# Making the low parts of the mixer's weight tiles on GpSimd in place of VectorE

## The reference, cut to what matters

```python
h = h + FFN_RES * swiglu(rmsnorm(h, ffn1_norm[layer]), ffn1_w_gate[layer], ffn1_w_up[layer], ffn1_w_down[layer])
h = h + token_mixing(rmsnorm(h, mix_norm[layer]), w_in[layer], lb_all[layer], hg_norm[layer],
                     conv_w[layer], conv_b[layer], conv_ln_g[layer], conv_ln_b[layer], w_out[layer])
h = h + FFN_RES * swiglu(rmsnorm(h, ffn2_norm[layer]), ffn2_w_gate[layer], ffn2_w_up[layer], ffn2_w_down[layer])
...
def token_mixing(u, ...):
    z = u @ w_in
    ...
    o = gla_chunk_scan(qs, ks, vs, gs)
    ...
    glu = z[..., 5 * W:5 * W + C] * jax.nn.sigmoid(z[..., 5 * W + C:5 * W + 2 * C])
    c = depthwise_conv(glu, conv_w, conv_b)
    ...
    return jnp.concatenate([hg_out, c], axis=-1) @ w_out
```

## Time and profile before

| | |
|---|---|
| median of 3 runs | 2802.3 us (2797.23, 2802.3, 2803.67) |
| span of the profiled execution | 2799.2 us, first to last instruction |
| a time of its own for the profiled execution | none is listed beside the three; its span is 3.1 us under their median |
| one pass of the loop over heads | about 157 us, three passes from about 1108 to 1580 us |
| low parts made in the four heads | 28 of the 171 in the program |

### The profile page before, as it was taken

One profiled execution on the slowest core, in us unless ns is written; L12 is line 12 of the kernel. 1 busy time (PEld: TensorE's weight loads), 2 busy tenths in 40 slices (PEclk: granted clock), 3 DMA queues, 4 the chain that ended last, 5 costly groups with the idle time before them and its releaser, 6 DMA issues.

```text
span 2799.2 us, 31878 instructions
## 1 busy us (share of the span) xinstructions
PE 2635.1 (94%) x13699; PEld 2232.0 (80%) x13699; DVE 1331.7 (48%) x1217; ACT 554.6 (20%) x599; POOL 23.1 (1%) x48
## 2 busy tenths in 40 slices
PE   7999999999999999898989779999999999999996
PEld 6888888888888878787878667788888888888884
DVE  4323343233432468877778775533333233333334
ACT  5111111111111132222322333311111111111114
POOL 0000000000000000000000000000000000000000
PEclk9999999999999999999999789999999999999998
DMA  4111111111111121010110201101111111111101
GB/s 130 38 38 39 38 38 35 35 39 38 38 39 31 57 80 46 21 45 26 31 33 33 97 29 57 43 31 38 38 39 38 39 38 38 39 38 31 38 23 75
DMA packets 146064, 119.92 MB, mean 43 GB/s; under 512 B 3841, under 2 KB 127937, under 8 KB 145921
## 3 DMA queue, kind: packets, MB, share of 16 engines
q1 hardware_dynamic: 141312, 98.64, 11.5%
q0 software_dynamic: 4608, 19.04, 1.7%
HBM read 103.18 MB, written 14.48 MB: 42 GB/s over the span
## 4 chain that ended last, share of the span: by engine, by line
PE 81%; DVE 10%; issue 4%; ACT 3%; DVEq 0%; DMA 0%; ACTq 0%; SPq 0%
PE PS L425 75%; DVE H L1214 2%; PE PS L599 2%; DVE T L1207 1%; DVE T L1205 1%; ACT WH L823 1%; DVE COUT L1440 1%; PE PS L604 1%; DVE BF L1329 0%; DVE BB L1329 0%; PE PS L631 0%; DVE AB L1327 0%; DVE WL L1111 0%; PE PS L729 0%; ACT Q L959 0%
## 5 line engine op out<-in xcount | busy, mean ns | idle before, releaser
L425 PE MATMUL PS<-XH,WH 128*128 128x512 f32 (+2 forms) x2976 | 763.0, 365 | 30.3 <-DVE XL L1172 12.1
L425 PE MATMUL PS<-XL,WH 128*128 128x512 f32 (+2 forms) x2976 | 750.2, 360 | 0.0
L425 PE MATMUL PS<-XH,WL 128*128 128x512 f32 (+2 forms) x2976 | 748.0, 360 | 0.0
L425 PEld LDWEIGHTS PS<-XH,WH 128*128 128x128 f32 x2976 | 499.0, 190 | 122.5 <-issue 27.4
L425 PEld LDWEIGHTS PS<-XL,WH 128*128 128x128 f32 x2976 | 500.4, 190 | 88.9
L425 PEld LDWEIGHTS PS<-XH,WL 128*128 128x128 f32 x2976 | 497.8, 190 | 88.1
L1214 DVE SCALAR_TENSOR_TENSOR H<-PS,H 128x1296 f32<-128x1296 f32 (+1 forms) x176 | 263.6, 1498 | 209.3 <-PE PS L425 209.3
L425 PE MATMUL PS<-HH,WH 128*128 128x512 f32 (+2 forms) x1056 | 269.1, 363 | 29.9 <-DVE H L1214 25.2
L1111 DVE TENSOR_TENSOR WL<-WR,WH 128x1024 fp32r<-128x1024 f32 (+1 forms) x171 | 205.6, 1203 | 185.4 <-ACT WH L823 185.3
L823 ACT ACTIVATE WH<-WR 128x1024 fp32r<-128x1024 f32 (+1 forms) x171 | 176.4, 1032 | 488.7 <-PE PS L425 474.7
L425 PE MATMUL PS<-HH,WL 128*128 128x512 f32 (+2 forms) x1056 | 264.6, 359 | 0.0
(11 more groups left out here) (210 smaller groups left out, 1272.4 us busy)
## 6 DMA issues: line engine op xcount, KB each, us to landing
WR<-in_ffn_w_gate SPq DMA_DIRECT2D x44, 512.0 KB, 3.7
WR<-in_ffn_w_up SPq DMA_DIRECT2D x44, 512.0 KB, 3.8
WR<-in_ffn_w_down SPq DMA_DIRECT2D x44, 512.0 KB, 3.5
WR<-in_w_in SPq DMA_DIRECT2D x28, 512.0 KB, 3.9
hsave<-H POOLq DMA_DIRECT2D x8, 648.0 KB, 3.2
XT<-in_x_sample SPq DMA_DIRECT2D x8, 512.0 KB, 10.6
out_sample<-XO SPq DMA_DIRECT2D x8, 512.0 KB, 5.4
H<-hsave POOLq DMA_DIRECT2D x5, 640.0 KB, 4.2
```

The source lines that it names most:

```text
L425: mm = nc.tensor.matmul(SET[s][:, o:o + b - a], wt[:, wat[0], wat[1]:wat[1] + P], x(a, b), start=first and wt is WH and x is xh, stop=last ...
```

## The change

VectorE's `split` in `head` becomes a count only, and GpSimd's queue makes those 28 low parts with `low_weights`, each after `split_hi` of its slot and raising the same `split_lo`. The two saves of the loop, which had a loop of their own on GpSimd's queue, now stand among them: `save_c` of head i-1 after the second low part of pass i, `save_y` of head i-1 after the seventh. The low parts of the two feed-forward networks and of the output projection stay on VectorE.

```diff
-            with pool.Fori(0, EARLY) as i:
-                save_c(i)
-                save_y(i)
+            uses = [Count() for _ in range(RING)]
+            for s in range(RING):
+                uses[s].add(3 * NF // RING)
+            uses[HEAD_SLOTS[0]].add()
+
+            def low_weights(pos):
+                s = (HEAD_SLOTS + HEAD_SLOTS[0:1])[pos + 1]
+                uses[s].add()
+                pool.wait_ge(split_hi[s], uses[s].now())
+                nc.gpsimd.tensor_tensor(WL[:, s, :], WR[:, s, :], WH[:, s, :].bitcast(F32),
+                                        ALU.subtract).then_inc(split_lo[s], 1)
+
+            for pos in range(7):
+                low_weights(pos)
+            with looped(pool, 1, HEADS, head_counts(uses)) as i:
+                for pos in range(7):
+                    low_weights(pos)
+                    if pos == 1:
+                        save_c(i - 1)
+                save_y(i - 1)
...
                     if z and slot % 2 == 0:
-                        split((HEAD_SLOTS + HEAD_SLOTS[0:1])[pos + 1])
+                        uses[(HEAD_SLOTS + HEAD_SLOTS[0:1])[pos + 1]].add()
```

## The result

The changed kernel takes 2811.04 us (median of 5 runs, 2809.42 to 2812.62), the kernel before 2801.99 in the runs beside it (5 runs, 2797.23 to 2803.67). The ratio is 1.004, 95% interval 1.0029 to 1.0051: slower by about 9 us, where I had forecast 3.0 and counted that as no change. It lies inside the range, just past the forecast's own upper end of 2810.7 and short of the 2813.7 of the rival in which the conflict also costs the clock.

The account below looks back on a forecast made before the run. TensorE is busiest over the span (94%), but in a loop pass it waits on VectorE's queue. Positions 2 and 4 (+1.1 each), 1 and 3 (-0.6 each) give 1.0 us a pass, 3.0 in three: 2802.3 to 2805.3; range 2785 to 2818.

Parts of the forecast that it names:

- no change: Whole kernel: differences within about 0.2%, 5.6 us, cannot be told apart; the forecast 3.0 lay inside; chance of between 0.36.
- the forecast's own upper end: Whole kernel: 2810.7 us, from a GpSimd subtraction of 2.65 us, +8.4 over three passes.
- the rival in which the conflict also costs the clock: Behind position 2: a wait past about 3.1 us halves the clock, 2.8 us a pass; +11.4, 2813.7; chance 0.25.
- What a low part costs is its place: VectorE's queue: low parts delay work TensorE waits for; removal alone saves 4.85 us a pass, 14.6 in three.
- The conflict at its upper end: VectorE's instructions with two SBUF inputs: the next one stands still for GpSimd's whole 2.2 us; forecast +3.0, chance 0.35.
- positions 1 to 4: Loop pass: 1.1 us later at positions 2 and 4, 0.6 earlier at 1 and 3; 1.0 longer a pass.
- GpSimd's length: Each low part on GpSimd: taken as 2.2 us, ends 1.8 and 2.65; every 0.1 us counts 1.2 in all.
- Positions 5, 6, 0: the idle time takes it. Zero.: Behind these low parts VectorE idles for TensorE (1.65, 0.15, 0.96 us), so nothing is gained or lost there.
- Without it everything behind starts 1.13 us earlier: Position 2: with the low part gone from VectorE's queue, TensorE's wait of 2.54 us falls by 1.13.
- the case without conflict: Rival: GpSimd's reads do not hold VectorE, or only use its gaps; -14.6 us, 2787.7; chance 0.27.
- The forecast without the clock: Loop: VectorE's standstill alone, no clock loss, 3.0 us over three passes, 2805.3; chance 0.35.

Follow-up runs that it names:

- kernel 1: The change with GpSimd's subtraction cut to one column of the 1024, queue, waits and semaphores kept: 2786.39 us, ratio 0.9952.
- kernel 5: The kernel before, with VectorE making the loop's low parts of positions 0 to 5 behind the recurrence's step instead of ahead of it: 2787.49 us, ratio 0.9952.
- kernel 11: The kernel before, unchanged, profiled once more for the granted clock: 2799.93 us, one time.
- 3: The change with only the low parts of positions 1 and 3 on GpSimd, VectorE making the others: 2798.68 us, ratio 1.000.
- 10: Kernel 5 with the doubling level at position 2 also put ahead of the convolution's first tap: 2777.31 us, ratio 0.9914.
- 2: The change with GpSimd subtracting one column and only writing zeros to the other 1023: 2786.62 us, ratio 0.995.
- 6: The change with GpSimd's loop subtractions also waiting for VectorE's doubling level (positions 1, 2, 3) or the query's product (position 4): 2788.18 us, ratio 0.9959.
- 9: Kernel 6 with GpSimd's subtraction at position 0 also waiting for VectorE's doubling level: 2786.29 us, ratio 0.9945.
- 4: The change with only the low parts of positions 2 and 4 on GpSimd, VectorE making the others: 2812.22 us, ratio 1.0039.
- kernel 7: The change with each of GpSimd's subtractions cut into four of 256 columns: 2805.34 us, ratio 1.0013.

## Why the prediction was right or wrong, point by point

- *What a low part costs is its place.* Right, and shown twice: with the work gone (kernel 1) idle time falls by 15.0 where 14.6 was worked out, with the work only moved back (kernel 5) by 14.3. That the sums are so near is in part luck: three times 0.4 too much at position 2 stands against 1.15 that was not counted at position 0. (The waits of the three passes were not alike to 0.02 us either: position 1 reads 1.63 in the first, and the second change of heads 3.67, with no releaser shown.)
- *The conflict at its upper end, and positions 1 to 4.* Right in mechanism and size, as the table shows: -0.64, +0.96, -0.69 and +1.04 for -0.6, +1.1, -0.6 and +1.1, and 2.97 us of idle time where the sum had 3.0. GpSimd's length, taken as 2.2, is 2.35 to 2.41 where nothing hinders it and 2.2 as VectorE feels it. The Trainium skill's figure (GPSIMD Engine Reference, Performance versus the Vector engine), 2.25 as an estimate, lies between the two.
- *"Positions 5, 6, 0: the idle time takes it. Zero."* Wrong for position 0 of the first pass. I read the idle time in the second pass (0.96 us of slack) and took the passes for alike. In the first pass TensorE waits there, 2.18 us before and 3.22 after. The slack came with the clock: in the pass I read it had just fallen to 0.50, and at full clock TensorE waits at position 0 in a later pass too (1.37 in kernel 11). Worth 1.04 us, once. It made up for what the other places fell short of 3.0, so the agreement of the sum is in part luck.
- *"Without it everything behind starts 1.13 us earlier" at position 2.* Too much, in the case without conflict: the wait fell from 2.54 to 1.81, 0.73. The low part had covered the 0.30 us that the first tap waits for the gate's product, a wait that appears in the rows only now; and it had started 0.08 us before that product's end, which the tap, waiting for the product, does not.
- *The clock.* This is the step that failed. I set it beside the forecast as a rival that begins when the wait at position 2 passes 3.1 us, and gave it 0.25. The forecast without the clock has 3.0 us, the clock's part is 6 to 7, and that took the result out of "no change". The rival's price, 2.8 us a fall, was 1.9 to 2.1 in the 18 matmuls behind position 2. Its condition does not hold for a single fall: the clock fell there behind 1.81 (kernel 1) and behind 2.54 and 2.55 (kernels 11 and 3, once each), and held behind 3.50 in one pass of the change. For the sum of a kernel it fits:

| wait at position 2 | kernels | TensorE busy in the stretch | passes with a fall behind position 2 |
|---|---|---|---|
| 0.54 | 10 | 525.1 | 0 of 3 |
| 1.8 to 2.2 | 1, 2, 5, 6, 9 | 526.0 to 529.8 | 14 of 15 |
| 2.54 | before (two profiles), 3 | 528.4 to 529.6 | 2 of 9 |
| 3.45 to 3.50 | change (two profiles), 4, 7 | 535.0 to 541.3 | 10 of 12 |

The falls behind the shorter waits are short ones: the 18 matmuls take 4.4 to 5.1 us there, and 5.1 to 5.6 behind the long wait.

Shown: VectorE's stand-still, its unit (one instruction) and what it takes (GpSimd reads and two SBUF inputs); that lateness and hand-over cost nothing that these runs can tell; that the clock is lower in both profiles of the change, and in the two other kernels whose wait at position 2 is as long. It is not GpSimd's work as such: kernels 6 and 9 make the same 28 subtractions, without the long wait, and stay at 526.0 and 529.7. Not shown: what decides a single fall. Below 3.45 the wait does not order the kernels, and the sum of TensorE's idle time does not at all (kernel 7 idles less than the kernel before and has the lowest clock). Executions differ, too: the mean granted clock was 0.969 to 0.973 in the change's five runs and 0.972 to 0.977 in seventeen of the kernel before. No run held the waits and moved the clock alone, so how much of the 6 to 7 us the long wait itself causes, and how much is the chance of when the falls come, stays open.

## What to carry to other kernels

Before work is moved to GpSimd to relieve VectorE, look at what VectorE does in that moment: here a subtraction that reads SBUF stopped a VectorE instruction with two SBUF inputs for nearly its whole length (2.2 of 2.4 us) and cost nothing beside those that read PSUM. A semaphore that started it there turned a loss of 9 us into a gain of 13. Before moving anything, ask whether the place in the queue is the cost: here the same instruction behind the step that TensorE waits for gave 14 us with no second engine. And read every pass of a loop, the first above all, before a term is set to zero.

## What the runs showed of the hardware that I had not expected

- An instruction of 10 columns was held up as long as one of 640: 0.54 us beside a subtraction of 256 columns (kernel 7).
- VectorE's first tap, with one SBUF input, was held up by GpSimd's subtraction (1.7 us) and by its mere write (0.37 us).
- The granted clock fell to 0.50 behind waits of 1.81 us and held behind one of 3.50, so a wait's length does not foretell a single fall. Two executions of one kernel differ in where it falls, of the kernel before and of the change alike.
